# A plain first pair, spread norm steps and a shorter tile-by-tile end in two conv-FFN layers

## The reference

```python
x = layer_norm(DEEPNORM_ALPHA * x + g1 * (m @ w_out[l]), ln_g[l, 0], ln_b[l, 0])
u = layer_norm(x) * (1 + sc2) + sh2
f = conv_ffn(u, w_up[l], ffn_conv_w[l], ffn_conv_b[l], w_down[l])
x = layer_norm(DEEPNORM_ALPHA * x + g2 * f, ln_g[l, 1], ln_b[l, 1])

def conv_ffn(u, w_up, cw, cb, w_down):
    a, g = jnp.split(u @ w_up, 2, axis=-1)
    return (jax.nn.silu(depthwise_conv(a, cw, cb)) * g) @ w_down
```

## Time and profile before

| | us |
|---|---|
| median of 3 runs | 2892.37 (2891.76 to 2892.74) |
| the profiled execution, on the device | 2892.87 |
| its span in the profile | 2891.1 |
| TensorE busy | 2619.4 (91%) |
| VectorE busy | 1660.6 (57%) |
| ScalarE busy | 1086.0 (38%) |
| GpSimd busy | 434.7 (15%) |

### The profile page before, as it was taken

The page is one execution under the profiler, slowest core; times in us unless marked ns, Lnnn a source line. Parts: engine busy times, 40 slices in busy tenths (PEclk is TensorE's granted clock), DMA queues, the critical chain, the costliest instruction groups (busy, mean ns, idle before and its releaser), DMA issues. The chain is left out here.

```text
span 2891.1 us, 35791 instructions
## 1 busy us (share of the span) xinstructions
PE 2619.4 (91%) x13356; PEld 2317.4 (80%) x13356; DVE 1660.6 (57%) x2446; ACT 1086.0 (38%) x1730; POOL 434.7 (15%) x245
## 2 busy tenths in 40 slices
PE   5798999995999999897977899997799999999887
PEld 2486788675999999875656799976699999977666
DVE  3235777766766666446454333357666666634565
ACT  4423677554332333233443311135433233323332
POOL 1060687431000000002022000023000000000220
PEclk7899999997999999999988799998899999999999
DMA  9911000121322222444643311121222222154543
GB/s 332 316 35 57 7 1 1 64 83 44 91 69 68 68 68 72 148 166 156 212 140 142 113 44 65 58 88 66 60 77 82 68 68 68 54 194 150 196 148 136
DMA packets 209222, 294.44 MB, mean 102 GB/s; under 512 B 11513, under 2 KB 146661, under 8 KB 209119
## 3 DMA queue, kind: packets, MB, share of 16 engines
q1 hardware_dynamic: 205892, 284.62, 30.4%
q0 software_dynamic: 2736, 8.01, 0.7%
q10 hardware_dynamic: 491, 0.42, 0.0%
HBM read 247.73 MB, written 45.29 MB: 101 GB/s over the span
## 5 line engine op out<-in xcount | busy, mean ns | idle before, releaser
L2769 PE MATMUL ps<-d_ring,hs 128*128 128x512 f32 x2376 | 588.0, 408 | 76.8 <-DVE hs L1639 62.9
L2769 PEld LDWEIGHTS ps<-d_ring,hs 128*128 128x128 f32 x2376 | 462.0, 196 | 201.9 <-DVE hs L1639 70.8
L1639 DVE TENSOR_TENSOR d_ring<-d_raw,d_ring 128x1024 fp32r<-128x1024 f32 x132 | 173.0, 1310 | 296.8 <-ACT hs L1002 295.9
L2628 PE MATMUL ps<-act_a,w_A 128*128 128x384 f32 x1584 | 286.5, 340 | 13.6 <-ACT fp L1002 8.3
L2628 PE MATMUL ps<-act_b,w_A 128*128 128x384 f32 x1584 | 285.2, 339 | 13.5 <-ACT fp L1002 8.1
L2628 PEld LDWEIGHTS ps<-act_a,w_A 128*128 128x128 f32 x1584 | 279.4, 191 | 14.5 <-ACT fp L1002 8.8
L2628 PEld LDWEIGHTS ps<-act_b,w_A 128*128 128x128 f32 x1584 | 278.1, 190 | 14.3 <-ACT fp L1002 8.7
L981 POOL TENSOR_TENSOR ey<-ey,gb_end 128x1024 f32<-128x1024 f32 x15 | 35.7, 2381 | 1584.6 <-ACT ey L1458 1584.6
L2416 PEld LDWEIGHTS ps<-act_b,uw 128*128 128x128 f32 x1440 | 253.2, 191 | 2.4 <-issue 2.4
L2416 PE MATMUL ps<-act_b,uw 128*128 128x384 f32 x1440 | 254.6, 340 | 0.3 <-PE ps L2769 0.3
L1002 ACT ACTIVATE d_ring<-d_raw 128x1024 fp32r<-128x1024 f32 x132 | 139.5, 1057 | 266.5 <-PE ps L2769 184.4
(11 more groups left out here) (262 smaller groups left out, 4323.7 us busy)
## 6 DMA issues: line engine op xcount, KB each, us to landing
d_raw<-in_w_down SPq DMA_DIRECT2D x132, 512.0 KB, 3.4
ada_w<-in_w_ada SPq DMA_DIRECT2D x52, 512.0 KB, 6.5
h_rows<-fh SPq DMA_DIRECT2D x44, 576.0 KB, 3.6
h_raw<-h_rows SPq DMA_DIRECT2D x132, 192.0 KB, 3.9
raw_u<-in_w_up SPq DMA_DIRECT2D x44, 512.0 KB, 5.4
raw_odd<-in_w_up SPq DMA_DIRECT2D x44, 512.0 KB, 5.5
end_w<-in_w_ada SPq DMA_DIRECT2D x24, 512.0 KB, 5.7
late_w<-in_w_ada SPq DMA_DIRECT2D x20, 512.0 KB, 6.8
```

The costliest lines, as they stand in the source:

```text
L1639: return v.tensor_tensor(dst, src, hi.bitcast(F32), ALU.subtract)
L2628: mm = pe.matmul(o, w[:, a, k, :], m, start=first and (k, a, i) == (0, 0, 0), stop=last and (k, a, i) == (KH - 1, 1, 0), skip_group_check= ...
L2769: mm = pe.matmul(out, h[:, a, tile % 3 * P:(tile % 3 + 1) * P], d[:, w, 512 * half:512 * half + 512], start=f == 0 and (a, w) == (0, 0), s ...
```

## The change

Three edits, made together in both layers.

1. **First pair.** All three chunks are done with plain products of A11, A12, A21, A22, twelve products in place of eleven; `FIRST` replaces `ORDER0`. The token sums are no longer formed in `split` of tiles 3 to 5 but in `token_sums` on VectorE behind step 8; tiles 6 to 8 get a place of their own (`ln_v`), since `ln_u[0:2]` is needed for the sums. There is a fourth t operand, written over chunk 1 of the low half of the input. The turns of tiles 6, 7, 8 stand between the plain products. The raw weights of pair (0,1) are loaded after two t splits instead of three.
2. **Closing norm.** `stats1`, `norm1`, `stats2`, `norm2`, `modulate` and `split` are taken apart into single steps (`mean1`, `root1`, `inverse1`, `scale1`, `mean2`, `root2`, `inverse2`, `scale2`, `modulate`, `split`), one or more items apart; tile k begins at item 2 + 3k of a round. The evacuations are all at item 1 and go through an SBUF buffer `e_t`. The turns, end blocks and their loads move to other items. The last pair's work on ScalarE and VectorE is interleaved with items 0 to 2 (`last`).
3. **Round ends.** In rounds 0 and 1 one row instead of two is taken tile by tile.

```diff
-END_SPOTS = {39: 0, 60: 1}
+END_SPOTS = {NF + 7: 0, 2 * NF + 7: 1}
+END_FROM, END_GAP = 2, 3
+END_TURNS = {r * NF + END_FROM + END_GAP * k + 7: 3 * (r - 1) + k for r in (1, 2) for k in range(3)}
...
@@ SyncE @@
-                    sp.wait_ge(t_lo, 3 * (l + 1))
+                    sp.wait_ge(t_lo, 4 * l + 2)
                     self.raw(0, 1)
...
-                        if i in (NF + 18, 2 * NF + 15):
+                        if i in (2 * NF - 1, 3 * NF - 1):
                             self.rows(i // NF)
...
-                if i == 30:
+                if i == NF + 2:
                     for a in range(4):
                         end_unit(a)
-                elif i == 44:
+                elif i == NF + 14:
...
-                elif i == 64:
+                elif i == 2 * NF + 14:
...
@@ ScalarE @@
-                    if s == NT - 1:
-                        self.turned(0)
-                        self.turned(1)
-                        act.wait_ge(out_evac, NT * (l + 1))
-                        self.hi(0, 0, "S2")
-                        self.hi(0, 0, "A22")
-                    elif s == NT:
-                        self.turned(2)
-                        self.first_product(0, 0)
-                        act.wait_ge(t_lo, 3 * (l + 1))
-                        self.hi(0, 0, "S4")
-                        self.hi(0, 0, "A21")
+                    if s == NT:
+                        act.wait_ge(p_a, n + 2)
+                        act.wait_ge(pads, 2 * l + 1)
+                        self.line(0, B_A, p1_rdy)
+                        self.turned(0)
+                        self.turned(1)
+                    elif s == NT + 1:
+                        act.wait_ge(p_d, n + 2)
+                        self.line(1, B_D, a_ev)
+                        self.turned(2)
                         act.wait_ge(act_rdy, NT * (2 * l + 2))
+                        self.hi(0, 1, "A11")
+                        self.hi(0, 1, "A12")
+                        self.third(0, 0)
+                        self.turned(3)
+                        act.wait_ge(t_lo, 4 * l + 4)
+                        self.hi(0, 1, "A22")
+                        self.silu(0, 0)
+                        for x in ("S2", "S3", "S1", "S4"):
                             self.hi(0, 1, x)
...
+                def last(self):
+                    g, b = NG - 1, 1
+                    self.hi(g, b, "A21")
+                    self.third(g, b)
+                    self.first_product(g, b)
+                    self.down(0)
+                    self.down(1)
+                    self.first(g, b)
+                    self.silu(g, b)
+                    self.down(2)
+
+                def norm(self, t0, j):
+                    for k in range(3):
+                        s = j - END_FROM - END_GAP * k
+                        if s == 1:
+                            self.root1(t0 + k)
+                        elif s == 3:
+                            self.scale1(t0 + k)
+                        if self.l == 0:
+                            if s == 6:
+                                self.root2(t0 + k)
+                            elif s == 8:
+                                self.scale2(t0 + k)
+                            elif s == 11:
+                                self.modulate(t0 + k)
...
@@ VectorE @@
-                    if 3 <= tile < 6:
-                        before, here = ln_u[:, tile - 3, :], ln_u[:, tile, :]
-                        v.wait_ge(mod_done, tile + (NT * i4 + 1))
-                        v.tensor_tensor(before[:, 0:HW], here[:, 0:HW], before[:, 0:HW], ALU.subtract).then_inc(t_sum, 1)
-                        v.tensor_tensor(here[:, 0:HW], here[:, HW:D], here[:, 0:HW], ALU.subtract)
-                        v.wait_ge(act_hi, tile + (NT * i4 + 1))
-                        v.wait_ge(t_sum, 4 * l + tile - 2)
-                        lo(dest[:, KH:KD, 1, sl], halves(here[:, HW:D]), dest[:, KH:KD, 0, sl])
-                        lo(dest[:, 0:KH, 1, sl], halves(before[:, 0:HW]), dest[:, 0:KH, 0, sl]).then_inc(act_rdy, 1)
...
+                def token_sums(self):
+                    t3, t2, t4, t1 = (t_source(x) for x in range(4))
+                    chain(v.tensor_tensor(t1, t3, t1, ALU.subtract))
+                    chain(v.tensor_tensor(t3, t2, t3, ALU.subtract))
+                    chain(v.tensor_tensor(t2, t2, t1, ALU.subtract))
+                    v.tensor_tensor(t4, t4, t2, ALU.subtract).then_inc(t_sum, 1)
...
                     if s == NT - 1:
+                        self.token_sums()
+                    elif s == NT:
                         self.turned(0)
                         self.turned(1)
+                        self.taps(0)
+                    elif s == NT + 1:
+                        self.turned(2)
+                        self.lo(0, 1, "A11")
+                        self.lo(0, 1, "A12")
+                        self.turned(3)
+                        self.lo(0, 1, "A22")
+                        self.first()
+                        self.sums(0, 1)
+                        self.lo(0, 1, "S2")
+                        self.first_rest()
+                        for x in ("S3", "S1", "S4"):
                             self.lo(0, 1, x)
...
+                def last(self):
+                    g, b = NG - 1, 1
+                    self.lo(g, b, "A21")
+                    v.wait_ge(h_mul, NF * (self.l + 1) - 1)
+                    self.second(g, b)
+                    self.third(g, b)
+                    self.down(0)
+                    self.gate2(g, b)
+                    self.down(1)
+                    self.line(g, b)
+                    self.conv(g, b)
+                    self.down(2)
+                    self.rest(g, b)
+
+                def norm(self, t0, j):
+                    for k in range(3):
+                        s = j - END_FROM - END_GAP * k
+                        if s == 0:
+                            self.mean1(t0 + k)
+                        elif s == 2:
+                            self.inverse1(t0 + k)
+                        if self.l == 0:
+                            if s == 5:
+                                self.mean2(t0 + k)
+                            elif s == 7:
+                                self.inverse2(t0 + k)
+                            elif s == 12:
+                                self.split(t0 + k)
+
+                def evac(self, tile, rows):
+                    v.tensor_tensor(rows[:].rearrange("p (a n) -> p a n", a=2), banks(TILE_BANKS[tile]),
+                                    g_end[l][1 if tile == 0 else 0][:].rearrange("p (a n) -> p a n", a=2), ALU.mult).then_inc(dn_evac, 1)
+                    v.wait_ge(dn_evac, NT * l + tile + 1)
+                    chain(v.scalar_tensor_tensor(y, y, ALPHA, rows[:], ALU.mult, ALU.add))
...
-                            if j == 2:
-                                self.evac(t0)
-                                self.evac(t0 + 1)
-                            elif j == 3:
-                                self.evac(t0 + 2)
-                            if j in (3, 4, 5):
-                                self.stats1(t0 + j - 3)
+                        if r and j == 1:
+                            for k in range(3):
+                                self.evac(t0 + k, e_t[k % 2])
...
@@ TensorE @@
-                    self.p1(w)
-                    pe.wait_ge(act_rdy, rows + 6)
-                    self.p5(w)
+                    self.plain(B_A, w["A11"], w["A12"], p_a, 0, 2)
                     turn(6)
                     pe.wait_ge(out_evac, out + 8)
-                    pe.wait_ge(t_lo, 3 * l + 1)
-                    self.p7(w)
-                    pe.wait_ge(t_lo, 3 * l + 2)
-                    self.operands(0, 0, 5)
-                    self.p6(w)
+                    self.plain(B_B, w["A21"], w["A22"], p_b, 0)
                     turn(7)
-                    self.p2(w, n)
-                    pe.wait_ge(t_lo, 3 * l + 3)
-                    self.operands(0, 0, 6)
-                    self.p4(w, n)
-                    self.operands(0, 0, 7)
-                    self.p3(w, n)
+                    pe.wait_ge(act_rdy, rows + 6)
+                    self.plain(B_D, w["A11"], w["A12"], p_d, 1, 2)
+                    self.plain(B_E, w["A21"], w["A22"], p_e, 1, 2)
                     turn(8)
...
-                        rows = LAST_ROWS if r == 2 else 2
+                        rows = LAST_ROWS if r == 2 else 1
...
-                if i in (30, 33, 36):
-                    end_turn((30, 33, 36).index(i))
-                elif i in (52, 55, 58):
-                    end_turn(3 + (52, 55, 58).index(i))
-                elif i in END_SPOTS:
-                    end_block(END_SPOTS[i])
+                if i in END_TURNS:
+                    end_turn(END_TURNS[i])
+                elif i + 4 in END_SPOTS:
+                    end_block(END_SPOTS[i + 4])
```

310 lines of the change are left out of this document (141 added, 169 removed).

## The result

| | before | after |
|---|---|---|
| median, us | 2892.07 | 2761.96 |
| range, us (4 runs each) | 2889.19 to 2892.74 | 2759.36 to 2764.49 |
| ratio, 95% interval | | 0.9552 (0.9535 to 0.9568) |
| profiled execution; span, us | 2892.87; 2891.1 | 2763.77; 2762.0 |
| granted clock over the span, as a share of 2.4 GHz | 0.950 | 0.964 |

The change gains 130 us, 4.5%.

A forecast was written before the change was run, and what follows sets the result against it. TensorE was held bound by the ScalarE/VectorE norm chain in the first pair and their splitting of w_down and h in the rounds; 33 + 85.8 − 3.8 = 115.0 us off 2892.4 gave 2777.4 us, range 2763 to 2808.

The forecast's parts named there:

- the first pairs: Middle norm with the first up-projection pair: shorter norm chain, 16 us gained in layer 0 and 17 in layer 1.
- the rounds: Four down-projection rounds with norm work: stops of 88.8 us nearly all go, 85.8 us gained.
- the starts: Start of each down-projection: last store and item 3's load go out later, 1.9 us lost a layer, 3.8 in all.
- C: First pair and down-projection start: nothing given back in block (0,1), no loss at the start, 2755 to 2765 us; 8%.
- A: First pair gives nothing, VectorE's backlog returning as stops over several blocks: 2810 us, 2794 when half; 14%.
- B: Rounds: a third to a half of the stops stays, slack used up, 2806 to 2821 us; 12%.
- D: Items with a norm step: engines wait for each other in every one, slower, about 2990 us; 4%.
- E: Whole kernel: no change in time, because the end is set elsewhere; 2%.
- F: Evacuations at the rounds' start: held up by GpSimd, 4.4 us a round, 17.6 in four, 2795 us; 2%.
- given back: Block (0,1) behind the first pair: VectorE's postponed work returns as stops and low clock, 9.0 of 25.2 us.
- reserve of 3 us: Rounds: allowance for overlooked losses, 1 us in each round of layer 0 and 0.5 in layer 1.
- signs of being wrong: Rounds: hs waits every item from item 2; block (0,1) and successors each stopping before S2; ScalarE's table loads multiplying.

The follow-up runs named there:

- e1: The kernel before with only the first-pair edit made, the down-projection schedule left as it was: 2850.14 us, ratio 0.9855.
- e8: The kernel after with SyncE's loads for items 3 and 4 issued ahead of the last store and item 5's right behind it: 2740.83 us, ratio 0.9473.
- e5: The kernel before with GpSimd's two closing operations of the last norm on 8 of the 1024 columns only: 2852.56 us, ratio 0.9856.
- e4: The kernel after with root and scale of a norm again in one item with mean and inverse: 2791.20 us, ratio 0.9661.
- e3: The kernel after with two rows instead of one taken tile by tile at the end of rounds 0 and 1: 2762.53 us, ratio 0.9554.
- e7: The kernel after with the last row's closing gating ahead of the third down-projection split on VectorE: 2754.50 us, ratio 0.9518.
- e10: The early-loads kernel with token sums behind tile 8's second statistics and t operands released after their own sums: 2737.25 us, ratio 0.9458.

## Why the prediction was off by 15 us, step by step

**The sizes failed, not the mechanisms.** Two terms of the sum were too small, the first pairs (33 us, measured 41.7) and the rounds (85.8 us, measured 92.2); the terms for the starts and for what lies elsewhere were off by less and in part against each other. Of the rivals, C has the time (2755 to 2765), but not by its mechanism: block (0,1) does give 6.7 us a layer back, and a little is lost at the start. A, B, D, E and F did not come true. Term by term:

| term | forecast | measured |
|---|---|---|
| first pairs | 16 + 17 | 20.5 + 21.2 |
| rounds | 85.8 | 92.2 |
| starts of the down-projections | −3.8 | −1.6 |
| elsewhere | 0 | about −3 |

**The first pair.** This is the step that failed most. The chain was right in its order, and its time was lost in two places, the norm steps and the part given back. With the 3.38 us off, the evacuation of tile 8 starts at 649.6 (forecast 651.3), the token sums end at 669.3 (670.3), the last split ends at 681.7 (683.3), block (0,1) starts at 691.6 (693.5): 27.2 us ahead of the 718.8 of before, where 25.2 were forecast. Of these 2.0 us 1.7 stand in the first link: the three steps from the evacuation of tile 5 to that of tile 8 took 32.2 us (620.80 to 653.01 in the trace), 10.7 each, where the forecast added up 11.3. TensorE, named as the bound, was done before (at 649.95 in the trace) and bound nothing. The four sums err the other way, 9.2 us where 8.6 were taken, and not evenly: 3.95 us for the one that lay beside a GpSimd operation, 1.76 for the others, so 2.3 on the mean. Then "given back" was 9.0 us in the forecast; it is 6.7 (29.6 us from block (0,1) to pair (1,0), 22.9 before). The stop before S2 is 3.06 (3.7), that before product 3 is 1.60 (2.9), the rest is low clock, 2.0 (2.4). Together 4.3 us a layer. e1 gives the same 41.6 us by itself, so nothing of it hangs on the rounds.

**The rounds.** Forecast were 99.4 and 93.7 us, measured are 97.3 and 92.6. The losses of 88.8 us went completely, and 3.4 more. The reserve of 3 us "for what I overlook" was not needed, and the base was too high: 396 matmuls take 92.3 us and not 92.9, since the 46.46 us of the earlier trace rows for 198 were doubled (92.9 against the 92.27 of one stretch of 396). About 0.2 of that is the drain of the last matmul (its row ends after the next could have begun), counted twice, and the rest is that this row was itself 0.2 us slower than the same 198 in e8 (46.28); the three turns and the end block cost 4.6 to 4.8 us and not 5.2 (a turn's row says 1.03 us, but the next row starts 0.79 behind it). The cause holds in both halves that it named: e5 takes away the stretching and gets 38 us back, e4 puts back the hand-over within an item, with the stretching that falls on it, and loses 26 to 29. They are not parts of one sum, for the reason given with e5. What the prediction did not see is that they weigh differently by layer, 8 us of stretching in 28.0 and 29.5 lost in a layer 0 round, 11 in 16 in a layer 1 round. Rival B needed affine steps and statistics to fall together and use up the slack; in the kernel after splits are still stretched, and no stop follows.

VectorE, then GpSimd, in the second round of layer 0 of the kernel after:

```profile
1287.53 1.23 DVE L2160 SCALAR_TENSOR_TENSOR ey<-ey,et 128x1024 f32<-128x1024 f32 x1
...
1306.05 2.75 DVE L1675 TENSOR_TENSOR hs<-h_raw,hs 128x384 fp32r<-128x384 f32 x1
```

```profile
1305.12 3.26 POOL L995 TENSOR_TENSOR ey<-ey,gb_end 128x1024 f32<-128x1024 f32 x1
```

The split of 0.55 us stands for 2.75 until the GpSimd operation, begun before it, has ended at 1308.4. The Trainium skill (SBUF — State Buffer, Who interferes with whom) says that such a pair excludes each other for a whole instruction; the trace agrees with it, 2.2 us here. The new second half of the evacuation, for which rival F feared the same, has no GpSimd operation beside it and takes its 1.23 us.

**Edit 3** had no term of its own in the sum, only bank times, and e3 shows that beside the early evacuations it is worth nothing that can be measured.

**The start.** Item 3 was forecast 1.9 us later a layer and came 0.4 and 1.2 later; the store itself ends 1.5 us later in layer 0, counted from pair (1,0). The forecast of TensorE's stop, "8 to 10 us", was just missed by the 7.85 that it is. That the store of the last pair sets it was right: e7 shortens the chain and gets 7.5 us, e8 cuts it and gets 21. The prediction priced this stop as a small loss and took it for given; it was the largest thing left to gain.

**Elsewhere.** The execution that was profiled ran 3.4 us longer ahead of the middle norm. The first plain product starts at 649.95, 647.60 and 646.98 in the traces of the kernel after, e8 and e10, which have the same code up to there, so this is scatter and no effect of the change.

**The signs.** TensorE's waits between the last out-projection and the second pair are 14.5 us, inside the 13 to 19 that were named; no wait for hs is left inside a round, block (0,1) stops before S2 and its successors don't, and ScalarE loads a table nine times in both traces. So none of the signs of being wrong appeared; the range failed on sizes alone.

**The range.** Its low edge took in only the upper part of C's 8%. The reserves were all put on one side (1 and 0.5 us a round), while nothing in the rows said that the errors would lie on that side. The chances of a sign, 0.94 for faster, stood on firm ground: two stages with idle time that was seen, measured and had a cause.

## What to carry to other kernels

- When engines take their instructions in order and share a ring of operands, put every step that waits for another engine at least one item behind the step that feeds it. Steps of several tiles may share items; hand-overs within one item cost TensorE here 8 us on 97 in a round with two norms, with GpSimd's operations over the splits behind them.
- Before a stage whose operands are loaded, look at what stands ahead of its loads in the issuing queue. A store that waits for the last product cost 7.85 us and 2.0 us of low clock a layer, for loads that did not depend on it.
- A stop costs more than its length, and filling part of an idle stretch may give back less than the part, if the low clock then reaches further into the work behind it. When a chain is forecast link by link, keep the reserves out of the sum and in the range.

## What the runs showed of the hardware

- The same instruction, 1536 columns in and out of SBUF, took 3.95 us beside a GpSimd operation and 1.75 to 1.76 us without, in the same place of the program (e10 has it at 1.75 when it comes after the GpSimd operation).
- GpSimd's second closing operation took 3.26 us in the first tile of the second round of layer 0, while VectorE's splits ran beside it, and 2.40 in the two others, where it was VectorE's split that stood (3.34 us for 1.23). The loser of such a meeting is either engine.
- Behind an idle stretch of 6.5 us, 24 matmuls of 384 columns took 5.74 to 5.86 us, at full rate 4.33. Behind 9.13 us they took 7.22 us in one layer and behind 9.14 us 5.76 in the other: the same gap can cost 1.4 or 2.9 us.
